# A fused two-block kernel: three weight remainders ahead of the second recurrence move from GpSimd to VectorE

## What is computed

```python
h = rmsnorm(x, mix_pre_g[l])
q_a, f_a, i_a, g_a, q_b, k_b, v_b, f_b, gates = jnp.split(h @ w_in[l], IN_OFFSETS, axis=-1)
o_a = hgrn2_chunkwise(q_a..., f_a..., i_a..., lb_all[l])   # f = lb + (1-lb) sigmoid(f_a), q = silu(q_a)
```

## Time and profile before

| | |
|---|---|
| median of 3 runs | 1210.65 us (1206.61 to 1211.4) |
| the profiled execution's own time | 1210.9 us |
| span of its trace | 1209.1 us |
| TensorE busy | 1155.1 us, 96% |
| GpSimd busy | 888.3 us, 73%, of it 882.8 us in 724 remainder operations |
| ScalarE, VectorE busy | 593.1 us, 468.2 us |
| mean granted TensorE clock | 0.993 of full speed |
| mixing stage, slabs f1/0 to gt0/0 | from 584.5 to 749.1 us of the span |

### The profile page before, as it was taken

How to read it: one execution, slowest core, us unless ns; L and a number is a source line. 1 busy time by engine, 2 the same in 40 slices (tenths; PEclk the granted TensorE clock), 3 DMA queues, 4 the chain that set the end, 5 groups by cost and what they waited for, 6 DMA issues and landing times.

```text
span 1209.1 us, 21098 instructions
## 1 busy us (share of the span) xinstructions
PE 1155.1 (96%) x8438; PEld 983.0 (81%) x8438; DVE 468.2 (39%) x802; ACT 593.1 (49%) x867; POOL 888.3 (73%) x733
## 2 busy tenths in 40 slices
PE   7999899999999999999999989999999999999997
PEld 7899788777777888788997887887788988888785
DVE  5527655764554111101416576634433133111102
ACT  6364532533655454534554544465546456444533
POOL 4678954431177888798699998779876757888794
PEclk9989999999999999999999999999999999999999
DMA  9887533332175666566465554454776535665563
GB/s 339 275 272 209 138 91 89 111 118 89 41 239 163 194 184 191 174 189 191 116 186 140 144 138 140 129 150 140 226 244 192 157 100 163 191 186 182 170 197 102
DMA packets 182896, 202.08 MB, mean 167 GB/s; under 512 B 7528, under 2 KB 141072, under 8 KB 182032
## 3 DMA queue, kind: packets, MB, share of 16 engines
q1 hardware_dynamic: 177584, 185.78, 51.5%
q10 hardware_dynamic: 5216, 14.97, 3.7%
HBM read 196.51 MB, written 4.21 MB: 166 GB/s over the span
## 4 chain that ended last, share of the span: by engine, by line
PE 66%; POOL 17%; issue 7%; DVE 5%; ACT 5%; DMA 1%; ACTq 0%; DVEq 0%; POOLq 0%
PE ps L724 18%; PE ps L726 17%; PE ps L725 17%; POOL wlo L2700 17%; PE ps L721 12%; PE ps L729 2%; ACT whi L1337 1%; DMA raw<-in_w_in 1%; DVE x L1913 1%; DVE oblo L1905 1%; ACT L1337 1%; DVE red L2368 0%; DVE gt L1905 0%; ACT rl L1337 0%; ACT ps L1337 0%
## 5 line engine op out<-in xcount | busy, mean ns | idle before, releaser
L2700 POOL TENSOR_TENSOR wlo<-raw,whi 128x256 fp32r<-128x256 f32 (+1 forms) x724 | 882.8, 1249 | 304.9 <-ACT whi L1337 304.0
L1337 ACT ACTIVATE whi<-raw 128x1024 fp32r<-128x1024 f32 x324 | 340.9, 1057 | 306.5 <-PE ps L726 279.1
L724 PE MATMUL ps<-whi,hThi 128*128 128x512 f32 (+1 forms) x656 | 262.6, 400 | 8.3 <-POOL wlo L2700 6.1
L726 PE MATMUL ps<-whi,hTlo 128*128 128x512 f32 (+1 forms) x656 | 254.6, 388 | 0.0
L725 PE MATMUL ps<-wlo,hThi 128*128 128x512 f32 (+1 forms) x656 | 254.0, 387 | 0.0
L724 PE MATMUL ps<-hThi,whi 128*128 128x256 f32 x568 | 167.2, 294 | 11.7 <-POOL wlo L2700 5.8
L725 PE MATMUL ps<-hTlo,whi 128*128 128x256 f32 x568 | 161.8, 285 | 0.0
L726 PE MATMUL ps<-hThi,wlo 128*128 128x256 f32 x568 | 161.6, 285 | 0.0
L724 PEld LDWEIGHTS ps<-whi,hThi 128*128 128x128 f32 x656 | 123.3, 188 | 38.5 <-issue 11.5
L726 PEld LDWEIGHTS ps<-whi,hTlo 128*128 128x128 f32 x656 | 123.2, 188 | 26.0
L725 PEld LDWEIGHTS ps<-wlo,hThi 128*128 128x128 f32 x656 | 123.5, 188 | 22.1
(11 more groups left out here) (394 smaller groups left out, 1577.7 us busy)
## 6 DMA issues: line engine op xcount, KB each, us to landing
raw<-in_w_in SPq DMA_DIRECT2D x120, 512.0 KB, 3.7
raw<-in_ffn_w_in SPq DMA_DIRECT2D x176, 256.0 KB, 3.1
raw<-in_ffn_w_down SPq DMA_DIRECT2D x44, 512.0 KB, 4.2
raw<-in_w_mkv SPq DMA_DIRECT2D x16, 512.0 KB, 6.3
raw<-in_ada_w SPq DMA_DIRECT2D x8, 512.0 KB, 6.5
raw<-in_w_o SPq DMA_DIRECT2D x8, 512.0 KB, 4.4
raw<-in_w_branch_a SPq DMA_DIRECT2D x8, 512.0 KB, 3.7
raw<-in_w_branch_b SPq DMA_DIRECT2D x8, 512.0 KB, 4.1
```

What stands on the lines that cost most here:

```text
L724: e.matmul(o, l[0], r[0], start=start, stop=False)
L726: return e.matmul(o, l[1], r[0], start=False, stop=stop)
L1337: return e.activation(o, i, f, **k)
L2700: p = e.tensor_tensor(wlo[c % NHL][:, o], raw[i % NRAW][:, o], whi[c % NHL][:, o], ALU.subtract)
```

## The change

Three more slabs have their remainder made by VectorE: the second slab of hq1, the second slab of hq3, and the second slab of i0.

```diff
-BY_VECTOR = {"mv0": [2]}
+BY_VECTOR = {"hq1": [1], "hq3": [1], "i0": [1], "mv0": [2]}
```

## The result

The changed kernel takes 1220.58 us (median of 4 runs, 1218.22 to 1221.96) against 1209.35 us for the kernel before (4 runs, 1206.61 to 1211.4): ratio 1.0097, 95% interval 1.0075 to 1.0118. That is slower by more than 0.5%, the side to which 0.08 was given, and outside the range. The profiled execution took 1218.22 us, with a span of 1216.4 and a mean granted clock of 0.989.

A forecast was written before the change was run, and what follows sets the result against it. POOL was taken as the bound from about 634 to 750 us. Terms 0.0 - 0.8 + 0.3 - 0.5 = -1.0 us against 1210.9 gave 1209.9, as median 1209.7; range 1204.5 to 1215.

The forecast's parts named there:

- the side to which 0.08 was given: Whole kernel: slower by more than 0.5%, over 1216.7 us, chance 0.08.
- The three remainders: hq1/1, hq3/1, i0/1: 8.3 us leave POOL and come back whole as idle time; sum 0.0 us, bounds -0.2 and +1.5.
- The shift of the order: From `start hgrn`: planner's clock 1.2 higher, later steps one half unit later, two from fb on; terms -0.8, +0.3, -0.5 us.
- the term of -0.8 in the sum: At 649.87: `whi` of i1/3 comes ahead of group 0's exponential, so POOL goes on at once, -0.8 us.
- -0.5 for all this: Around fb: waits 0.49 and 0.83 may vanish or move, two DVE pairs (1.8 us) leave POOL's tight stretch; -0.5 us.
- three new waits of the size of the worst, 0.83 each: Shifted order: bound on the slower side, +2.5 us.
- wrong in another way: Sign of a wrong prediction: a difference over 2 us that arises outside 605 to 760.
- Lead kept: Ahead of POOL's tight stretch: POOL enters 5.6 us earlier, PE gains that, 1205.0, with the order's 3.9 1201.1; chance 0.10.
- Exponential holds back `whi`: ACT, groups 2 to 13: shifted exponential makes POOL wait, 0.6 to 0.7 us a group, +8, 1219 us; chance 0.08.
- DVE late for PE: hq1/1, hq3/1, i0/1: DVE waits for POOL's operation, 3 x 0.74, +2.2 us without the order's gain, 1212.9; chance 0.10.

The follow-up runs named there:

- the run with the sized filler: Changed kernel plus idle matmuls (11, 8, 7 and 11) fitted into PE's waits at kb1/1, gt0/2, step 52 and gt2/2: 1214.18 us, 1.0055 against the kernel before.
- the kernel with all three repairs: Changed kernel with `decay` behind step 24, fox step 18 behind ga1's second sigmoid half, step 44 behind gt0/0's first half: 1207.44 us, 1.0002 against the kernel before.

## Why the prediction was wrong

**The three remainders: right.** Net 0.0 was said, the run with before's order measured 0.9998 and a lag of 0.3 to 0.4. POOL's 8.3 us came back whole, as the prediction had it, but not whole as idle time: 6.0 us are idle time that ends with `whi` (7.16 us up to i0/3 instead of 1.12), and 2.3 are three lengthened operations. And POOL started i0/3, the first slab for which PE waits, within 0.1 us. PE's 0.0, 0.1 and 0.2 were 0.0, 0.0 and 0.2. One detail differs: POOL does not stand idle until DVE's remainder ends, it starts beside it and its first operation takes long (1.50 us at 610.92 and at 622.49, 1.49 at 628.32, against 0.74 alone), so that a slab took 3.58 us instead of 2.8. The rule from the Trainium skill, SBUF — State Buffer, section "SBUF: two separate sides", that the one which starts first has the ports for its whole instruction, agrees with the trace here to 0.14 us: DVE's operation ran on for 0.90 us behind POOL's start at all three places (610.60 + 1.22 - 610.92, 622.17 + 1.22 - 622.49 and 628.00 + 1.22 - 628.32), and POOL's first operation was longer by 0.76. It changed no sum, as said.

**The shift of the order: right as a shift, its gain of 0.8 not.** Steps 0 to 5 stand where the prediction worked them out, one half unit later, and two from fb on. The idle 0.82 at 649.87 is gone, but the term of -0.8 in the sum was not gained: the exponential of group 1 now waits 4.36 us for DVE (656.09) and stands ahead of the `whi` of qb1/0, POOL stands idle for 0.82 there, and the lag is 0.3 at qb1/1 as it was at i0/3. The exponential of group 2 came later, but by 1.0 us and not 1.8 (662.24 + 2.17 against 663.38 of the earlier trace rows), and the `whi` behind it by 0.5.

**What the shift is worth: the step that failed.** The prediction took "-0.5 for all this", with +2.5 as the bound on the bad side, from "three new waits of the size of the worst, 0.83 each". Measured is +9.7 for the order alone (with the 1.0 of the half clock at i0/3). Three things were wrong in that step.

1. It followed the shifted steps against the `whi` of ACT alone, and ended at 750. The recurrence's steps also change places with items that do not shift. `decay` stands in the hand-written list, ahead of kb1/0, with 3.7 us of DVE in a chain; before, step 24 stood just ahead of it. The planner's lines show it:

```
ahead of          before              after
kb0/1, half 1     hgrn 24             hgrn 23
kb1/0, half 0     decay, hgrn 25      decay
kb1/0, half 1     hgrn 26             hgrn 24
kb1/1, half 0                         hgrn 25
```

2. It did not follow the second chain. `fox` shares the clocks with `hgrn`, so its steps move too, and in ga1 one of them came between two sigmoids, with table loads of 1.28 us around it, and held back the `whi` of gt2. That is outside 605 to 760, the region to which the prediction had bound itself: its own line "wrong in another way" is what happened.

3. A wait of PE was counted once. Behind each of the three long ones the clock fell to 1.2 GHz for 3.4 us. By the run with the sized filler that was 3.3 of the 9.6 us.

The bound itself was a mistake of kind: a wait already in the trace says how large the waits of that order are, and nothing about those of another order.

**The rivals.** *Lead kept*: no; POOL had none to keep. *Exponential holds back `whi`*: its 1219 lies near the result, but not by its mechanism. It named the qb and kb slabs over twelve groups at 0.6 to 0.7 each. There the lag did not grow (0.3 at qb1/1, 0.0 at kb0/0), though the idle 0.82 at 658.18 is of its kind. The mechanism cost PE something once, at gt0/2, with group 13, as one wait of 2.0 us, where the kernel before has it with 0.73 at gt0/1. *DVE late for PE*: no, 0.2 us.

The account of the lag of 9.6 us, by the table of first matmuls and the repairs: 0.9 by v1/0 (0.3 by the remainders, the rest by `decay`; moving it brings -0.4, so it is worth 1.3), 4.5 from there to ga0/0 (step 44 and its `whi`, and a wait of 1.80 us for step 52), 4.3 from there to ba0/0 (step 18 of fox; with it moved, 0.6 to 0.7 arise there). The wait for step 52 still stands, at 1.77, in the kernel with all three repairs, and is paid there by what went away in ba1/0. What of the 4.5 belongs to step 52 and what to step 44 was not tried alone.

## What to carry to other kernels

A cost that is added to a planner's clock is a change of the whole order behind it. Before weighing it, lay out both orders, list every item that changed places with another, on all chains and to the end of the stage, and look for a fixed item or a table load that now stands between a step and its user; a change that adds an operation of 1.2 us can be made without that (the same operations in the old order cost nothing that the times show). A repair is judged at the place that it repairs: here one of them won more than half of its gain at another place, behind a table load that nobody had planned. And where a wait of TensorE comes near 2 us, as here, the slow matmuls that may follow it belong to its price.

## What the runs showed of the hardware

- In the kernel after, the granted clock was 0.50 for 3.4 us behind waits of PE of 2.79, 2.00 and 2.81 us, beginning 0.4 to 0.8 us after PE had started again; behind the one of 1.80 it stayed at 1.00. The longest wait in window 694 to 850 of the kernel before is 1.69 us, and its clock is 1.00 throughout.
- The same wait is not always followed by it. With the `decay` moved, the clock stayed up behind the 2.0 at gt0/2 and fell behind the 1.80 for step 52. The wait in ba1/0 (2.12 to 2.14 us, 2.26 in one) stands in fifteen of the eighteen profiles; the half clock follows in ten of them. The wait ahead of i0/3 is 1.45 to 1.48 us in the six profiles with the recurrence's start as before, never with half clock behind it, and 1.79 to 1.88 in the other twelve, with half clock in seven. Where it came, the lag at qb1/1 was 1.0 larger (1.3 against 0.3 with the changed kernel's remainders, 1.0 against 0.0 with those of before). So one profile differs from the next by 1 us and more for this reason alone, and a single trace is not enough to say what such a wait costs.
- Behind the waits of 2.78 to 2.82 us at kb1/1 the clock fell in all seven profiles that have them, behind those of 2.81 at gt2/2 in all five. In the two profiles with idle matmuls in these waits it fell at neither. At gt0/2 and ahead of step 52 it stayed up too with the sized filler, but there it does so at times without one.
